# Prologue reordered, scratch stores moved into the prologue and two periods, y stores on GpSimd's queue, in an eight-core encoder layer

## The chip, the cores and the metric

One Trainium2 chip, all 8 of its cores. Every core runs the same program on two prompt streams (2 x 4096 rows) and two sample streams (32 rows in all), without exchange between cores. The metric is the device time of one execution, that of the slowest core, in microseconds (us).

## The reference, cut to what matters

```python
def trunk_layer(x, ..., cache_k, cache_v):            # D_MODEL 1024, one layer
    h = rms_norm(x, n_pre_mix)
    z = h @ w_in                                      # 1024 -> 5632: q | k | v | u,v of gMLP | gate_a | gate_b
    q, k, v, zg, ga, gb = split(z)
    a = sink_attention(q, k, v)                       # 64-row chunks see 2 previous chunks and their own, 16 heads, 4 KV heads
    u, gv = split(gelu(zg), 2)
    gv = layer_norm(gv, ln_g, ln_b)
    bm = u * (tril(w_s) @ gv + b_s)                   # over chunks of 128 rows, 4 channel groups
    merged = sigmoid(ga) * (a @ w_attn_proj) + sigmoid(gb) * (bm @ w_gmlp_proj)
    x = x + rms_norm(merged @ w_out, n_post_mix)
    h2 = rms_norm(x, n_pre_ffn)
    g, up = split(h2 @ w_ffn_in, 2)                   # D_FF 2816
    x = x + rms_norm((silu(g) * up) @ w_ffn_out, n_post_ffn)
    return x, new_k, new_v, gv
```

All inputs and outputs are float32. The kernel multiplies in bfloat16 with float32 accumulation.

## The kernel before, in words

**Work.** A core's prompt rows are 16 tiles of 512 rows (4 blocks `b` of 128); the 32 sample rows are a seventeenth small tile, `smp`. `big` holds a tile's activations transposed, in 48 chunks of 128 features x 512 rows: C_H (normed input, 0), C_U (8), C_Q (16), gates C_GA and C_GB (24, 32), C_MG (40); the FFN activations take over 24 and up.

**Stages.** The loop over tiles (lines 1074 to 1183) is skewed: iteration i does, for tile i, the merge (16 units of 8 matmuls: attention projection with `s_wap`, gMLP projection with `s_wgp`), `s_wout`, the post-mix norm, FFN in and FFN out, and for tile i+1 the input norm, q/k/v, attention (spread between FFN units), u, gv, layer norm, the spatial gate, and the two gates. What tile 0 needs of these (and `smp`) is done ahead of the loop, in the prologue (lines 1029 to 1072): norm, q/k/v units, then gate units with attention spread over a planned span of 46 us, then gv of blocks 0 and 1, the u units, gv of blocks 2 and 3 and of `smp`, layer norm and spatial gate. A unit is 8 matmuls of 128x512 into one PSUM bank (UNIT = 1.71).

**Order.** Every piece of work is an event with a planned time: `dense` for matmul units, `ev` for the rest, both in `plan`. The list is sorted by that time and then emitted; it fixes the order of the instructions on every engine and in every queue, since each runs its own in order. Times are never waited for; waits come from the dependencies that `MK` tracks (lines 48 to 132).

**Weights.** 34 blocks of 128x8x512 (keys `s_win` 0 to 10, `s_wfi` 0 to 10, two each of `s_wap`, `s_wgp`, `s_wout`, and six `s_wfo`) pass through a ring of 6 slots. `wload` (367 to 388): use number n of a key loads the float32 input from GpSimd's queue with a cast to bfloat16 while n <= `store_use[key]`; at n == `store_use[key]` SyncE's queue also stores the slot to a bfloat16 scratch in HBM, a DMA that waits for the load's landing; later uses load the scratch from SyncE's queue. A next load is emitted when a block's last use frees its slot (lines 1193 to 1197). Lines 350 to 365 set `store_use` by position in the order of use, cyclically from (0, 2, 1, 3, 1, 2), plus 1 for `s_win`, whose first use is the prologue; LAST_CAST is 3.

**Queues.** SyncE: scratch loads and stores, all loads of x, constants. GpSimd: cast loads, and DMAs of `YQ`. `YQ` (421) is the queue that stores y and small outputs: ACT until the end of iteration LAST_CAST, then GpSimd (line 1180). From there on `TQ` is true too: `norm_T` (469) transposes the normed rows by a DMA from ACT's queue, in place of 8 PE transposes into bank 0 and a copy by ACT. x of tile i+2 is loaded 18 planned us after `fo_fin` of the block (line 1149) into the slot of `xt` from which y was stored, so its DMA waits for that store.

**Attention.** `plan_attn` (651) makes for each pair (block, half of the heads) events for scores and exp (`attn_S`: ACT reads banks 1 and 2 into `PT`), `attn_PV` (590: matmuls into BO and BD, DVE adds the sinks into `dent`), two reciprocals of 128x256 on DVE (626), and `attn_fin` (631), a DVE multiply that reads BO and so frees it for the next pair.

**Result.** `fo_fin` (904) adds the normed FFN output into `xt` in place (POOL for the first half, DVE for the second) and stores y from there.

**Start.** Line 970: ACT scales `gS[:, 0, :]`, after its load. Lines 972 to 974: GpSimd's queue loads the K/V cache, ahead of the first ring loads. `consts_a` (980) loads constants, among them the sinks, `w_s`, `bsB` and `b16`; `consts_use` (993) makes `bs16` from `b16` and `es2` on DVE, planned three units before the end of q/k/v.

## Time and profile before

| what | us |
|---|---|
| device time, median of 3 runs | 4430.7 (4227.88 to 4873.92) |
| the profiled execution: device time | 4223.91 |
| its span on the slowest core (core 7) | 4222.4 |
| spans of the 8 cores | 4210.5 to 4222.4 |
| busy on core 7: PE, DVE, ACT, POOL | 4081.1, 2029.5, 1720.8, 1273.3 |

The span is from the first to the last instruction of one core. PE is TensorE's matmul, PEld its weight load, DVE VectorE, ACT ScalarE, POOL GpSimd, SP SyncE; SPq is SP's queue. PEclk is TensorE's granted clock, 1.00 being the higher of its levels (2.4 GHz), 0.5 the lower (1.2 GHz); a mean lies between. q0 is the queue of GpSimd's DMAs, q1 that of SyncE's, q10 that of ACT's. A DMA's bytes are those it writes, so a cast load of a 2 MB float32 block counts 1 MB.

### The profile page before, as it was taken

How to read it: one execution, taken by the hardware profiler on the slowest of the kernel's cores; microseconds unless marked ns; L12 is line 12 of the kernel's file. 1: busy time of each engine (PE TensorE's matmuls, PEld its weight loads, DVE VectorE, ACT ScalarE, POOL GpSimd, SP SyncE). 2: the span in 40 equal slices, each digit the busy share in tenths (PEclk: the TensorE clock that was granted, in tenths of full speed). 3: DMA queues.
4: the chain of work that ended last, by engine and by line, in shares of the span. 5: the costliest groups of instructions: out<-in, count | busy, mean ns of one | idle time of the engine just before them, and what ended most of it. 6: DMA issues, size and time to landing. Idle time of an engine off the chain costs nothing.

```text
span 4222.4 us, 63031 instructions; the slowest of 8 cores (4210.5 to 4222.4 us)
## 1 busy us (share of the span) xinstructions
PE 4081.1 (97%) x20672; PEld 1836.0 (43%) x20672; DVE 2029.5 (48%) x2849; ACT 1720.8 (41%) x3385; POOL 1273.3 (30%) x1294
## 2 busy tenths in 40 slices
PE   6799899999999999999999999999999999999988
PEld 3344444444444444444444444444444444444444
DVE  3555353554545545454554545445454554545332
ACT  3453352543525344352433525344252534435232
POOL 0233332332223322322332233232322332232242
PEclk9899999999999999999999999999999999999999
DMA  9487978767465463645537364553635546364422
GB/s 167 102 162 144 215 176 189 207 169 222 148 211 156 152 193 117 217 142 185 160 132 217 123 205 147 180 169 133 211 129 189 158 151 193 118 217 143 166 91 96
DMA packets 197727, 696.94 MB, mean 165 GB/s; under 512 B 105121, under 2 KB 105698, under 8 KB 127778
## 3 DMA queue, kind: packets, MB, share of 16 engines
q1 hardware_dynamic: 80258, 535.68, 36.5%
q0 software_dynamic: 21744, 125.58, 15.7%
q10 hardware_dynamic: 95408, 31.67, 4.4%
q8 instruction: 174, 2.85, 0.3%
q14 instruction: 143, 1.17, 0.1%
HBM read 699.88 MB, written 69.99 MB: 182 GB/s over the span
## 4 chain that ended last, share of the span: by engine, by line
PE 82%; DVE 6%; DMA 4%; issue 3%; ACT 2%; POOL 2%; DVEq 0%; ACTq 0%; SPq 0%; POOLq 0%
PE ps L310 82%; DMA big<-hst 1%; POOL stt L327 1%; DVE tmpf L338 1%; ACT junk L317 1%; DVE stt L705 1%; DVE hst L338 1%; DMA tmpf<-b_s 1%; DMA xt<-xp 1%; DVE gvn L338 1%; DVE gvf L338 1%; DVE xt L327 1%; DMA ring<-s_wap 0%; DMA ring<-wgp 0%; PE ps L476 0%
## 5 line engine op out<-in xcount | busy, mean ns | idle before, releaser
L310 PE MATMUL ps<-big,ring 128*128 128x512 bf16 x12032 | 2682.0, 381 | 7.1 <-DMA ring<-s_wap 3.6
L310 PEld LDWEIGHTS ps<-big,ring 128*128 128x128 bf16 x12032 | 1151.3, 98 | 1441.2 <-issue 118.1
L310 PE MATMUL ps<-ring,big 128*128 128x512 bf16 (+1 forms) x5376 | 1143.0, 369 | 24.7 <-POOL big L327 11.5
L327 POOL TENSOR_TENSOR big<-tmpf 128x512 bf16<-128x512 f32 x480 | 621.8, 1295 | 1664.4 <-ACT tmpf L322 1069.4
L310 PEld LDWEIGHTS ps<-ring,big 128*128 128x128 bf16 x5376 | 518.4, 98 | 587.6 <-issue 44.4
L315 ACT ACTIVATE big<-ps 128x512 bf16<-128x512 f32 (+1 forms) x552 | 341.8, 627 | 621.6 <-PE ps L310 452.8
L338 DVE SCALAR_TENSOR_TENSOR tmpf<-tmpf,ps 128x512 f32<-128x512 f32 x352 | 241.9, 687 | 608.6 <-ACT tmpf L315 608.6
L315 ACT ACTIVATE y<-ps 64x256 bf16<-64x256 f32 (+3 forms) x1024 | 488.6, 478 | 56.6 <-PE ps L310 3.0
L629 DVE RECIPROCAL dent<-dent 128x256 f32<-128x256 f32 (+1 forms) x264 | 441.2, 1692 | 9.2 <-DVE dent L327 0.5
L338 DVE SCALAR_TENSOR_TENSOR tmpf<-big,ps 128x512 f32<-128x512 bf16 x256 | 175.4, 686 | 535.6 <-PE ps L310 533.9
L327 POOL TENSOR_TENSOR stt<-stt,negh 128x1 f32<-128x1 f32 x320 | 226.7, 710 | 605.0 <-DVE stt L331 443.1
L322 ACT ACTIVATE tmpf<-ps 128x512 f32<-128x512 f32 (+1 forms) x355 | 212.0, 597 | 321.9 <-PE ps L310 198.6
L315 ACT ACTIVATE tmpf<-ps 128x512 f32<-128x512 f32 x352 | 210.1, 597 | 286.4 <-PE ps L310 279.9
L317 ACT ACTIVATE junk<-ps 128x512 bf16<-128x512 f32 x260 | 155.2, 597 | 408.8 <-PE ps L310 341.2
L317 ACT ACTIVATE junk<-xt 128x1024 bf16<-128x1024 f32 (+1 forms) x130 | 137.1, 1054 | 351.0 <-DVE tmpf L338 247.4
L315 ACT ACTIVATE gvf<-ps 128x512 f32<-128x512 f32 (+1 forms) x130 | 77.5, 597 | 381.5 <-PE ps L310 380.0
L705 DVE BATCH_NORM_STATS2 stt<-gvf 128x6 f32<-128x512 f32 (+1 forms) x130 | 87.8, 687 | 261.9 <-ACT gvf L315 261.9
L327 POOL TENSOR_TENSOR big<-tmpf,big 128x512 bf16<-128x512 f32 x128 | 146.7, 1160 | 210.3 <-DVE tmpf L327 210.1
L338 DVE SCALAR_TENSOR_TENSOR hst<-xt,stt,gS 128x1024 bf16<-128x1024 f32 (+1 forms) x130 | 167.5, 1289 | 59.0 <-DMA big<-hst 37.0
L327 POOL TENSOR_TENSOR xt<-xt,tmpf 128x512 f32<-128x512 f32 (+1 forms) x130 | 165.4, 1272 | 97.5 <-DVE tmpf L338 97.4
L327 DVE TENSOR_TENSOR xt<-xt,tmpf 128x512 f32<-128x512 f32 (+1 forms) x130 | 160.8, 1237 | 14.6 <-DVE tmpf L338 1.6
L338 DVE SCALAR_TENSOR_TENSOR tmpf<-ps,stt,gS 128x512 f32<-128x512 f32 (+1 forms) x195 | 140.0, 745 | 21.5 <-POOL stt L327 21.2
(94 smaller groups left out, 1550.4 us busy)
## 6 DMA issues: line engine op xcount, KB each, us to landing
ring<-s_wfi SPq DMA_DIRECT2D x148, 1024.0 KB, 6.0
ring<-s_win SPq DMA_DIRECT2D x138, 1024.0 KB, 5.9
ring<-s_wfo SPq DMA_DIRECT2D x54, 1024.0 KB, 4.9
ring<-w_in POOLq DMA_DIRECT2D x38, 1024.0 KB, 13.7
xt<-xp SPq DMA_DIRECT2D x64, 512.0 KB, 12.1
ring<-s_wap SPq DMA_DIRECT2D x29, 1024.0 KB, 10.7
ring<-wfi POOLq DMA_DIRECT2D x28, 1024.0 KB, 10.0
ring<-s_wout SPq DMA_DIRECT2D x27, 1024.0 KB, 6.4
```

The costliest lines, as they stand in the source:

```text
L310: m.op(PE, lambda e: e.matmul(out, lhsT=lhsT, rhs=rhs, start=start, stop=stop), reads=reads, writes=[("ps", b)])
L315: m.op(ACT, lambda e: e.activation(out=out, in_=in_, func=func, scale=scale), reads=reads, writes=writes)
L317: m.op(ACT, lambda e: e.activation(out=out, in_=in_, func=func, scale=scale, accum_out=accum_out), reads=reads, writes=writes)
L322: m.op(eng, lambda e: e.activation(out=out, in_=in_, func=AF.Copy), reads=reads, writes=writes)
L327: m.op(eng, lambda e: e.tensor_tensor(out=out, in0=in0, in1=in1, op=op), reads=reads, writes=writes)
L338: m.op(eng, lambda e: e.scalar_tensor_tensor(out=out, in0=in0, scalar=scalar, in1=in1, op0=op0, op1=op1), reads=reads, writes=writes)
L629: m.op(DVE, lambda e: e.reciprocal(out=dv, in_=dv), reads=[("dent", n % 2, h)], writes=[("dent", n % 2, h)])
L705: m.op(DVE, (lambda hh: lambda e: e.bn_stats(out=stt[0:P, c + 6 * hh:c + 6 * hh + 6], in_=gvf[0:P, g, hh * 512:(hh + 1) * 512]))(hh), read ...
```

## The change

- `store_use`: 8 keys (`s_win` 3 to 6, `s_wap`, `s_wgp`) are stored at their first use, 9 in iteration 0, the other 17 in iteration 1. LAST_CAST becomes 1; with it line 1180 sets `TQ` (DMA transposes) two iterations earlier.
- `YQ` is GpSimd's queue from the start.
- Prologue: attention is planned over the gate units' span alone; ACT copies BO to `tmpf` after PV, and POOL multiplies from there; gv of two blocks is followed by four u units, twice, with gv of `smp` before the last four; layer norm is placed after each gv block, the spatial gate after the u units that it multiplies. Normed gv of blocks 2 and 3 goes to `hst`, that of `smp` to `junk`. Copies after the transposes of blocks 1 and 3, and the gate multiplies of those blocks, go to DVE.
- `gS[:, 0, :]` is scaled on DVE, planned after the first two blocks' statistics. The cache loads are an event of the plan, and so stand behind the first six ring loads.

`fo_fin`, which adds in place, is not touched.

```diff
-        use_order = [(w, cb) for cb in range(2) for w in ("s_wap", "s_wgp")] + [("s_wout", 0), ("s_wout", 1)]
...
-        STORE_PERIOD = (0, 2, 1, 3, 1, 2)
-        LAST_CAST = max(STORE_PERIOD)
+        keys = [(w, cb) for w in ("s_wap", "s_wgp", "s_wout") for cb in range(2)]
+        keys += [(w, cb) for w in ("s_win", "s_wfi") for cb in range(11)]
+        keys += [("s_wfo", n, c) for n in range(2) for c in range(3)]
+        LAST_CAST = 1
+        in_prologue = {("s_win", cb) for cb in range(3, 7)} | {(w, cb) for w in ("s_wap", "s_wgp") for cb in range(2)}
+        in_first = {("s_wout", 1), ("s_win", 0), ("s_win", 2), ("s_wfi", 2), ("s_wfi", 5), ("s_wfi", 8),
+                    ("s_wfo", 0, 1), ("s_wfo", 1, 0), ("s_wfo", 1, 2)}
...
-            n = STORE_PERIOD[o % 6] + (1 if key[0] == "s_win" else 0)
+            n = 0 if key in in_prologue else (0 if key in in_first else LAST_CAST) + (1 if key[0] == "s_win" else 0)
...
-        YQ = [ACT]
+        YQ = [POOL]
         TQ = [False]
+        PRO = [True]
...
-            act(t["big"][:, c0:c0 + 8, b * P:(b + 1) * P], pTv[:, 0:8 * P].rearrange("p (k t) -> p k t", k=8), AF.Copy,
-                [("ps", pT_b)], BK(t, c0, c0 + 8, (b,)))
+            tcopy(DVE if PRO[0] and b % 2 else ACT, t["big"][:, c0:c0 + 8, b * P:(b + 1) * P],
+                  pTv[:, 0:8 * P].rearrange("p (k t) -> p k t", k=8), [("ps", pT_b)], BK(t, c0, c0 + 8, (b,)))
...
+            if PRO[0] and not sample:                      # end of attn_PV
+                ti = ntmp()
+                t["ao"][n] = ti
+                tcopy(ACT, tmpf[:, ti, :], banks[BO][:, :], [("ps", BO)], [("tmpf", ti)])
...
+            if n in t["ao"]:                               # attn_fin
+                ti = t["ao"][n]
+                tt(POOL, a_out, tmpf[:, ti, :].rearrange("p (g q) -> p g q", g=4),
+                   dv.rearrange("p (g q) -> p g q", g=4), ALU.mult,
+                   [("tmpf", ti), ("dent", n % 2, 0), ("dent", n % 2, 1)],
+                   BK(t, C_Q + 4 * tp, C_Q + 4 * tp + 4, (b,)))
+                return
...
+        def gn_of(t, b):                                   # where the normed gv of a block lies
+            g = b % 2
+            if t["sample"]:
+                return junk[:, :], ["junk", "junk"]
+            if t["own"] == 0 and b >= 2:
+                return hst[:, g, :], [("hst", g)] * 2
+            return gvn[:, g, :], [("gvn", g, 0), ("gvn", g, 1)]
...
-            tt(PX[0], uv, tmpf[:, ti, :].rearrange("p (j t) -> p j t", j=nj), uv, ALU.mult, [("tmpf", ti)] + uk, uk)
+            px = DVE if PRO[0] and b % 2 else PX[0]
+            tt(px, uv, tmpf[:, ti, :].rearrange("p (j t) -> p j t", j=nj), uv, ALU.mult, [("tmpf", ti)] + uk, uk)
...
-        act(gS[:, 0, :], gS[:, 0, :], AF.Copy, [("gS", 0)], [("gS", 0)], scale=32.0)
         m.fence([POOL], [k for b in range(4) for k in xk(b)])
-        for s_ in range(2):
...
+        def load_cache():
+            for s_ in range(2):
...
+        ev(0.0, load_cache)
+        ev(2.2, lambda: ts(DVE, gS[:, 0, :], gS[:, 0, :], 32.0, None, ALU.mult, None, [("gS", 0)], [("gS", 0)]))
...
-        e_at = plan_attn(t, s0 + 0.1, 46.0, smp)
-        u_end = now[0] + 12 * UNIT + 8 * SC
-        for b in range(2):
-            for hh in range(2):
-                dense(gv_unit(t, b, hh), UNIT)
-            plan_ln(t, b, now[0], u_end + 0.1 + 2.0 * b)
-        both(u_units(t), u_units(smp), 8)
-        for b in range(2, 4):
-            for hh in range(2):
-                dense(gv_unit(t, b, hh), UNIT)
-            plan_ln(t, b, now[0])
-        for hh in range(2):
-            dense(gv_unit(smp, 0, hh), UNIT)
-        e_sp = plan_ln(smp, 0, now[0] + 2.0)
+        e_at = plan_attn(t, s0 + 0.1, now[0] - s0, smp)
+        uu, us = u_units(t), u_units(smp)
+        for k in range(2):
+            for b in (2 * k, 2 * k + 1):
+                for hh in range(2):
+                    dense(gv_unit(t, b, hh), UNIT)
+                ev(now[0] + 0.1, (lambda b: lambda: ln_a(tiles[0], b))(b))
+                ev(now[0] + 2.1, (lambda b: lambda: ln_b_step(tiles[0], b))(b))
+            if k:
+                for hh in range(2):
+                    dense(gv_unit(smp, 0, hh), UNIT)
+                ev(now[0] + 0.1, lambda: ln_a(smp, 0))
+                ev(now[0] + 2.1, lambda: ln_b_step(smp, 0))
+            both(uu[4 * k:4 * k + 4], us[4 * k:4 * k + 4], 4)
+            for b in range(2 * k + 2):
+                if k == 0 or b >= 2:
+                    ev(now[0] + 0.1 + 0.2 * b, (lambda b: lambda: spatial(tiles[0], b, 0))(b))
+                if k == 1:
+                    ev(now[0] + 1.1 + 0.2 * b, (lambda b: lambda: spatial(tiles[0], b, 1))(b))
+        ev(now[0] + 2.0, lambda: spatial(smp, 0, 0))
+        e_sp = now[0] + 2.1
         ev(now[0], consts_b_use)
         not_before(max(e_at, e_sp) + 0.1)
+        ev(now[0], lambda: PRO.__setitem__(0, False))
```

## Rows read from the trace of the kernel before

**Rows 1.** The page, part 1: busy us (share of the span) xinstructions

```profile
PE 4081.1 (97%) x20672; PEld 1836.0 (43%) x20672; DVE 2029.5 (48%) x2849; ACT 1720.8 (41%) x3385; POOL 1273.3 (30%) x1294
```

**Rows 2.** Windows: start:end, length, busy of each engine (x), PEclk, DMA share, GB/s

```profile
21.50:68.20 46.70, 36.77 (x284) 20.04 (x284) 11.27 (x27) 18.18 (x40) 1.59 (x3) 1.00 1.02 168
68.20:152.00 83.80, 67.12 (x400) 28.29 (x401) 49.27 (x70) 48.71 (x108) 4.00 (x8) 0.85 0.66 142
152.00:191.50 39.50, 27.93 (x206) 13.90 (x203) 22.80 (x39) 11.81 (x24) 13.34 (x16) 0.85 0.53 90
191.50:264.00 72.50, 68.55 (x372) 33.41 (x370) 36.53 (x55) 26.05 (x48) 29.94 (x33) 0.97 0.75 134
...
378.00:648.70 270.70, 256.51 (x1283) 115.53 (x1282) 125.90 (x173) 111.39 (x210) 89.08 (x97) 0.98 0.86 183
648.70:912.95 264.25, 254.46 (x1280) 114.50 (x1278) 125.01 (x173) 111.04 (x210) 83.79 (x87) 0.99 0.79 195
912.95:1170.35 257.40, 253.10 (x1281) 114.25 (x1280) 124.71 (x173) 110.83 (x210) 77.68 (x76) 1.00 0.59 177
...
1672.07:3929.33 2257.26, 2240.99 (x10935) 998.57 (x10934) 1122.38 (x1550) 926.41 (x1812) 680.97 (x650) 1.00 0.51 166
```

**Rows 3.** Timeline of the prologue: start, length, instruction [idle before <-what ended it]

```profile
14.36 1.28 ACT L315 ACT_TABLE_LOAD   x1 [14.36 <-DMA gS<-g]
...
31.98 3.33 PE L310 MATMUL ps<-big,ring 128*128 128x512 bf16 x8
...
66.22 0.21 DVE L324 CAST bs<-tmpf 1x128 bf16<-1x128 f32 x1 [8.11 <-DMA tmpf<-b_s]
...
68.23 0.59 PE L310 MATMUL ps<-y,ones 128*64 128x512 bf16 x2 [3.83 <-DVE Vt L324]
...
190.87 0.18 PE L310 MATMUL ps<-WmT,gvn 32*128 32x32 bf16 x1 [6.45 <-DVE gvn L324]
```

**Rows 4.** Groups by form on ACT, 60 to 165 us: busy us, mean ns

```profile
L315 ACT ACTIVATE y<-ps 64x512 bf16<-64x512 f32 x28 | 16.5, 590 | 1.8 <-PE ps L310 0.3
...
L315 ACT ACTIVATE y<-ps 64x256 bf16<-64x256 f32 x28 | 10.6, 378 | 2.8 <-PE ps L310 1.2
L315 ACT ACT_TABLE_LOAD x8 | 10.3, 1283 | 6.4 <-PE ps L310 3.3 <-issue 3.0
```

**Rows 5.** Groups by form on DVE, 60 to 165 us

```profile
L629 DVE RECIPROCAL dent<-dent 128x256 f32<-128x256 f32 x16 | 27.4, 1732 | 1.1 <-DVE dent L327 0.5
```

**Rows 6.** The page, part 5: nearest rows to the moved multiply and copy

```profile
L322 ACT ACTIVATE tmpf<-ps 128x512 f32<-128x512 f32 (+1 forms) x355 | 212.0, 597 | 321.9 <-PE ps L310 198.6
...
L327 POOL TENSOR_TENSOR big<-tmpf,big 128x512 bf16<-128x512 f32 x128 | 146.7, 1160 | 210.3 <-DVE tmpf L327 210.1
```

**Rows 7.** Timeline of PE in iterations 0, 1 and 2

```profile
209.50 0.61 PE L476 MATMUL ps<-ident,hst 128*128 128x128 bf16 x8 [0.41 <-DVE hst L338]
...
482.77 1.01 PE L476 MATMUL ps<-ident,hst 128*128 128x128 bf16 x8 [8.06 <-DVE hst L338]
...
741.73 3.42 PE L310 MATMUL ps<-big,ring 128*128 128x512 bf16 x8 [3.56 <-DMA ring<-s_wap]
```

**Rows 8.** Timeline of SP's queue, around the starts of iterations 1 and 2

```profile
429.35 0.33 SPq L141 DMA_DIRECT2D xt<-xp  x1
456.25 0.32 SPq L141 DMA_DIRECT2D s_wap<-ring  x1
456.77 1.70 SPq L141 DMA_DIRECT2D xt<-xp  x3
...
719.49 0.32 SPq L141 DMA_DIRECT2D s_wgp<-ring  x1
```

**Rows 9.** The page, part 3: queue: packets, MB, share of 16 engines' span

```profile
q1 hardware_dynamic: 80258, 535.68, 36.5%
q0 software_dynamic: 21744, 125.58, 15.7%
```

**Rows 10.** DMA from 400 to 420 us: a queue, and issues with median us to landing

```profile
q0 software_dynamic: 410, 2.82, 92.9%
...
ring<-w_in POOLq DMA_DIRECT2D x1, 1024.0 KB, 24.6
...
yp<-xt ACTq DMA_DIRECT2D x2, 512.0 KB, 18.0
```

More of the change, by code:

```diff
@@ L348, in reg @@
             f32_of[key], b16_of[key], store_use[key] = f, b, n
-        use_order = [(w, cb) for cb in range(2) for w in ("s_wap", "s_wgp")] + [("s_wout", 0), ("s_wout", 1)]
-        use_order += [("s_win", cb) for cb in range(3)] + [("s_wfi", cb) for cb in range(11)]
-        use_order += [("s_win", cb) for cb in range(3, 7)] + [("s_wfo", n, c) for n in range(2) for c in range(3)]
-        use_order += [("s_win", cb) for cb in range(7, 11)]
-        STORE_PERIOD = (0, 2, 1, 3, 1, 2)
-        LAST_CAST = max(STORE_PERIOD)
+        keys = [(w, cb) for w in ("s_wap", "s_wgp", "s_wout") for cb in range(2)]
[5 more added lines that the diff above has]
+                    ("s_wfo", 0, 1), ("s_wfo", 1, 0), ("s_wfo", 1, 2)}
         src_of = {"s_win": (w_in, s_win), "s_wfi": (wfi, s_wfi), "s_wap": (wap, s_wap), "s_wgp": (wgp, s_wgp),
                   "s_wout": (wout, s_wout), "s_wfo": (wfo, s_wfo)}
-        for o, key in enumerate(use_order):
+        for key in keys:
             f, b = src_of[key[0]]
-            n = STORE_PERIOD[o % 6] + (1 if key[0] == "s_win" else 0)
+            n = 0 if key in in_prologue else (0 if key in in_first else LAST_CAST) + (1 if key[0] == "s_win" else 0)
             if key[0] == "s_wfo":
@@ L720, in ln_b_step @@
                        ALU.mult, gk + [("st", c + 12), "lng"], gk)
-                dst, dk = (gvf, gk) if t["sample"] else (gvn, [("gvn", g, hh)])
-                stt_op(DVE, dst[0:P, g, cs], gvf[0:P, g, cs], stt[0:P, c + 15:c + 16], lnb[0:P, cs], ALU.mult,
+                nv, nk = gn_of(t, b)
+                dst, dk = (gvf[0:P, g, cs], gk) if t["sample"] else (nv[0:P, cs], [nk[hh]])
+                stt_op(DVE, dst, gvf[0:P, g, cs], stt[0:P, c + 15:c + 16], lnb[0:P, cs], ALU.mult,
                        ALU.add, gk + [("st", c + 15), "lnb"], dk)
@@ L725, in ln_b_step @@
                 m.dma(YQ[0], "st_gs", gs[:, :], gvf[0:P, g, :], reads=[("gvf", g, 0), ("gvf", g, 1)])
-                for hh in range(2):
-                    cs = slice(hh * 512, (hh + 1) * 512)
-                    tcopy(DVE, gvn[0:P, g, cs], gvf[0:P, g, cs], [("gvf", g, hh)], [("gvn", g, hh)])
+                tcopy(DVE, nv[0:P, :], gvf[0:P, g, :], [("gvf", g, 0), ("gvf", g, 1)], [nk[0]])
         def spatial(t, b, half):
@@ L736, in spatial @@
                 o = banks[b_][:, jj * P:(jj + 1) * P]
-                lhs = gvn[0:P, g, j * 128:(j + 1) * 128]
-                rk = [("gvn", g, j // 4)]
+                nv, nk = gn_of(t, b)
+                lhs = nv[0:P, j * 128:(j + 1) * 128]
+                rk = [nk[j // 4]]
                 if sample:
@@ L943, in build_program @@
             t["own"] = i % NT
-            for k in ("r", "ln", "wb", "sq", "fb"):
+            for k in ("r", "ln", "wb", "sq", "fb", "ao"):
                 t[k] = {}
```

5 lines of the change are left out of this document (2 added, 3 removed).

## The prediction, made before the changed kernel was run

> **What bounds the kernel now.** I read the page's busy times first. PE is busy 4081 of 4222 us [rows 1]: at most 141 us can be won by filling PE's gaps, so the question is where these lie. The windows by stage answer that. Nine iterations in the middle take 2257.26 / 9 = 250.8 us each, with PE busy 99% and the DMA engines 51% [rows 2]: nothing is to be had there, and the change leaves them alone. Iterations 1, 2 and 3 (cut at the first layer norm of the next tile) take 270.7, 264.25 and 257.4, that is 19.9, 13.4 and 6.6 above it, with DMA shares of 0.86, 0.79 and 0.59. The prologue runs from 21.5 to 191.5; in its last 123.3 us PE is busy 67.12 + 27.93 = 95.05, and at a mean granted clock of 0.85, so some 30% of that time lies at the lower level [rows 2]. The excess is thus in two places: about 40 us in three iterations, and PE idle or slow in the prologue.
>
> **Iteration 3 (and 2): TQ two iterations earlier.** Before, these two transpose on PE: 8 groups of 8 at 0.61 us [rows 7] are 4.9 us, the rest of the 6.6 is waiting around them. The DMA transposes that replace them run in all nine middle iterations, which include their price. Iteration 3 also loses its last 6 cast loads. It becomes a middle iteration: -6.6 (6 to 7).
>
> **Iteration 2.** Its 13.4 are the same 6.6 and a stall at the merge. SP's queue waited until 719.49 to store `wgp`, a block cast-loaded then [rows 8]; a scratch load of `s_wap` stood behind it, PE waited 3.56 us for that and ran the next 8 matmuls in 3.42 us, twice a unit, at the lower level [rows 7]: 5.3 us in all. After, no cast load or store is left in iteration 2. What comes late in its place: the stores of `s_win` 7 to 10 now all fall at the end of iteration 1, ahead of the scratch loads for this merge in SP's queue. If they hold as `wgp` did, up to 5.3 stays; I keep 2. -11.4 (8 to 13.4).
>
> **Iteration 1.** PE idles 8.06 us for the second block's norm [rows 7]. The cause is in SP's queue: x of block 0 goes out at 429.35, then the store of `s_wap` waits for its cast load until 456.25, and x of blocks 1 to 3 only goes behind it at 456.77 [rows 8]. After, `wap` and `wgp` were stored in the prologue, so four plain loads stand there, and the first store of iteration 1 (`wout` 0) comes behind the planned x loads. The PE transposes stay (6.6 above a middle iteration), so the floor is 257.4. I keep 1 us for late x: -12.3 (6 to 13.3).
>
> **DMA supply.** Cast loads: 11 in the prologue and 34, 28, 17, 6 in iterations 0 to 3 before (96); 11 and 30, 17, 0, 0 after (58). Stores: 6, 11, 11, 6 before; 4 in the prologue, then 13 and 17 after; 34 in both. Over the span q0 takes 0.157 x 4222 / 125.58 = 5.3 us of the DMA engines per MB, q1 0.365 x 4222 / 535.68 = 2.9 [rows 9]; under load a cast block takes 0.929 x 20 / 2.82 = 6.6 [rows 10]. With 4 MB of x and y, iteration 0 needs 30 x 5.3 + 4 x 2.9 + 13 x 2.9 + 11.6 = 220 us instead of 209, iteration 1 17 x 5.3 + 17 x 2.9 + 17 x 2.9 + 11.6 = 200 instead of 209. Both fit in some 257, so the stores hide, and iteration 0 is put at no gain or loss (0 to 2: at 191.5 it starts with the clock low, 0.97 over 72.5 us [rows 2], and my prologue still ends with a short wait). At 6.6 a cast load, iteration 0 would need 259, just full: the low end.
>
> **Prologue: start.** ACT's table load and first square wait 14.36 us for `gS`, and the first matmul of a unit starts at 31.98 [rows 3]. With the scaling on DVE, ACT squares x as it lands; then only `gS` (14.4) and its scaling (below 1.3) stand before the first scaled block, which saves the table load, a scaling and a square on ACT, and the copies alternate between ACT and DVE. I take 5 us. The ring's loads start ahead of the cache loads, 2.3 us earlier, so the weights follow; the cache comes behind six blocks, still ahead of its use. But DVE then waits for `b16` until 66.22, and PE for `Vt` behind it until 68.23 [rows 3]. The constants are issued when the norms are done, so I move that by the same 5: first PV at 63.2. If the constants don't land earlier (DMA share 1.02 in this window [rows 2]), the 5 us are lost here.
>
> **Prologue: the rest.** Before, a pair's PV could start only after two reciprocals of 1.73 us [rows 5] and the multiply that frees BO, with exps sharing ACT with gelu: 8 table loads, 10.3 us [rows 4]. After, an ACT copy (0.6) frees BO, a POOL multiply (1.2 to 1.3) follows off the path [rows 6], and attention ends with the gates: two table loads, -7.7 us. The copies add 8 x 0.6 = 4.8 to ACT, which still has 16 evictions of `t` and of `smp` and 27.1 us of exps [rows 4]: about 47 us for a phase that PE needs some 50 for, so ACT is late next there. The multiplies stand in POOL's queue ahead of the ring loads; each holds them as long as DVE is late with a reciprocal, a few us, against a ring of six. PE's work from first PV to merge: 95.05 busy, of which up to 30% of 123.3 = 37 us at the lower level; at full clock 95.05 - 18.5 = 76.5 if PE was busy all through these, 95.05 if never; I take 86. Of the 123.3 - 86 = 37 us lost, what stays? The tail: PE idles 39.5 - 27.93 = 11.6 in the last window [rows 2], most of all for the layer norm of `smp` (6.45 [rows 3]); four u units with `smp`'s (7.7 us) now stand between, which leaves 4, and I add 2 for banks held by queued DVE adds. Exps, reciprocals and the clock: 8. So the merge starts at 63.2 + 86 + 14 = 163, not 191.5: -28.3. Bounds: no gain at the start and 25 still lost, 68.2 + 86 + 25 = 179 (-12); 4 lost, 153 (-38).
>
> **The y stores.** Before, the first four tiles' stores went from ACT; each now costs POOL one issue and a wait for DVE's add, as in the middle iterations. "In-place result" changes nothing: `fo_fin` added in place before. The trace shows what waits on these stores: x of the tile after next needs the slot. At 400 to 420 a y store on ACT's queue took 18.0 us to land while q0 filled 92.9% of the engines, and a cast load in q0 24.6 [rows 10]. The Trainium skill, "DMA: Bandwidth & Descriptors", section on queues, rings and completion order, says that an engine takes turns between queue rows but consumes one row in ring order. By that rule a store in q0 stands behind the cast loads instead of sharing with them, which speaks against this move; the 18.0 against 24.6 agrees with it, and no row shows a y store in q0 beside cast loads.
>
> **Sum.** 28.3 + 0 + 12.3 + 11.4 + 6.6 = 58.6. Span 4222.4 - 58.6 = 4163.8, device time (1.5 above the span) 4165. Bounds: gains 12 + 0 + 6 + 8 + 6 = 32 give 4192, 38 + 2 + 13.3 + 13.4 + 7 = 73.7 give 4150. This is set against the profiled execution's 4223.91, near the lowest of the three runs shown (4227.88); their median, 4430.7, is 207 above it and no base for these rows.
>
> **Rivals.**
> A, late x. A y store in q0 lands like a cast load, 6.6 us later, x goes out as much later, and the stalls of iterations 1 and 2 stay whole, with SP's loads behind the x loads. For it: the 24.6. Against it: x of blocks 1 to 3 was 27 us late before, far more than 6.6. Gains 28.3 + 6.6 + 6.6: 4182.
> B, the prologue hardly gains, because ACT takes DVE's place: -12 instead of -28.3, 4181.
> C, slower. Stores wait in SP's queue for cast loads, and scratch loads behind them reach PE late: the 5.3 us that the store of `wgp` cost, at each of the 17 stores of iteration 1, is 90: 4165 + 90 = 4255. It decides above 58.6 / 5.3 = 11 such stalls. Against it: of 34 such stores before, two held PE up visibly, and iteration 1 has less DMA work than before.
> D, prologue at PE's floor: 63.2 + 76.5 = 140 (-51.8), and every other term at its end (35.7): gain 87.5, 4136.
>
> **How the numbers follow.** Forecast 0.66, A 0.11, B 0.11, C 0.04, D 0.08. The time is the forecast's, 4165. Its own range, 4150 to 4192, takes in A and B; for 8 in 10, and with rows of single executions, I reach to 4140 and 4210. About 2% (84 us, 4139) is what a measurement of this kernel can tell from no change. Faster by more: D, 0.08, and 0.01 of the forecast's low end. Slower by more needs over 4308, twice C's price: 0.02. Within 2%: 0.89.
>
> **What would show it.** Right: first unit near 27, first PV near 63, merge of tile 0 near 163 and two or three table loads in the attention; iterations 1, 2 and 3 near 258, 253 and 251; DMA transposes from iteration 2; no PE wait of over 4 us for a ring slot or x. Wrong: PV still waiting for DVE's reciprocals; iteration 1 above 265 with x behind y stores; SP's queue waiting over 20 us for cast loads with PE idle after it; iteration 0 longer, at a DMA share near 1.

## The result, and the profile after

| what | before | after |
|---|---|---|
| lowest device time, us | 4223.85 | 4182.72 |
| ratio after / before, 95% interval | | 0.9896 [0.9874, 0.9919] |
| the profiled execution, device time | 4223.91 | 4182.72 |
| its spans, slowest core (lowest) | 4222.4 (4210.5) | 4181.2 (4162.3) |

Some executions of any of these kernels take up to about 5000 us, with the cores of a die at a lower granted clock; only the others are compared here and below. The gain is 41 us, within 2%; the forecast was 58.6 and 4165, and the compared executions of the changed kernel took 4182.7, 4184.95 and 4185.4.

The page of the changed kernel, first line and part 1, beside [rows 1]:

```profile
span 4181.2 us, 62902 instructions; the slowest of 8 cores (4162.3 to 4181.2 us)
PE 4074.0 (97%) x20544; PEld 1828.4 (44%) x20544; DVE 2029.2 (49%) x2847; ACT 1697.0 (41%) x3368; POOL 1269.2 (30%) x1281
```

PE lost 128 matmuls (two iterations' transposes), but its busy time only 7 us: the gain is idle time. The windows by stage, core 4, columns as in [rows 2]; the cuts are the first PV (PE's first matmul with the attention's exps), the merge of tile 0, and the first layer norm of each next tile:

```profile
62.20:177.90 115.70, 97.76 (x623) 43.01 (x623) 67.23 (x100) 56.65 (x135) 24.04 (x27) 0.86 0.91 196
177.90:358.20 180.30, 176.51 (x896) 78.31 (x894) 91.68 (x113) 89.91 (x167) 63.88 (x68) 0.99 0.79 171
358.20:615.30 257.10, 253.08 (x1282) 114.23 (x1280) 124.84 (x173) 110.86 (x210) 85.58 (x90) 1.00 0.84 210
615.30:873.40 258.10, 252.53 (x1218) 111.54 (x1216) 125.55 (x173) 103.24 (x202) 78.47 (x77) 0.99 0.64 187
873.40:1123.80 250.40, 248.82 (x1218) 110.93 (x1216) 124.77 (x173) 103.02 (x202) 75.12 (x72) 1.00 0.51 166
```

Iterations 1 and 3 are where the forecast put them (257.1 for 258.4, 250.4 for 250.8). Iteration 2 took 258.1, not 252.8, and the merge starts at 177.9, not 163. That is one core. On core 2 the same stretch, first PV to merge, is 9.5 us shorter, with less PE busy time and a higher clock:

```profile
57.40:163.60 106.20, 91.25 (x623) 41.72 (x622) 66.94 (x100) 57.49 (x138) 24.02 (x27) 0.94 0.95 212
```

So all eight cores have to be read. The same marks on each core of both profiled executions, their means and the extremes (us):

| mark | before, mean (range) | after, mean (range) | change of the mean |
|---|---|---|---|
| first PV | 66.5 (65.5 to 68.2) | 58.7 (57.2 to 62.2) | -7.8 |
| first PV to merge | 121.0 (119.4 to 123.3) | 109.1 (106.2 to 115.6) | -11.9 |
| PE busy in it | 92.4 (90.4 to 95.1) | 92.8 (90.1 to 97.8) | +0.3 |
| iteration 0 (merge to layer norm) | 180.0 | 179.9 | -0.1 |
| iteration 1 | 269.2 (267.6 to 270.9) | 257.2 (257.1 to 257.7) | -12.0 |
| iteration 2 | 261.9 (257.5 to 264.6) | 254.4 (252.0 to 258.1) | -7.5 |
| iteration 3 | 257.5 | 250.8 (250.4 to 252.5) | -6.8 |
| the rest | 3059.1 (3058.1 to 3061.0) | 3058.8 (3054.9 to 3068.7) | -0.3 |
| span | 4215.2 | 4168.9 | -46.3 |

The stretch from first PV to merge doesn't hold quite the same work: by PE's records the changed kernel has 240 of the units' 128x512 matmuls in it (core 4), the kernel before 232 (core 7), one unit more, 1.7 us at the higher clock. The first PV comes a unit earlier in PE's order, and part of its 7.8 us is that.

The mean core gained 46.3; two cores stand out late after the change, core 4 (4181.2) and core 7 (4178.7), while six lie between 4162.3 and 4167.6, within 4 us of the forecast span of 4163.8. The time is the latest core's.

PE's timeline on core 4 beside [rows 3]:

```profile
26.37 3.59 PE L310 MATMUL ps<-big,ring 128*128 128x512 bf16 x8
...
62.24 0.50 PE L310 MATMUL ps<-y,ones 128*64 128x512 bf16 x2 [4.13 <-DVE Vt L324]
64.68 0.37 PE L657 MATMUL ps<-ident,ckb 128*128 128x128 bf16 x2 [1.40 <-DMA ckb<-ck]
70.63 0.37 PE L657 MATMUL ps<-ident,ckb 128*128 128x128 bf16 x2 [2.17 <-DMA ckb<-ck]
...
697.37 3.15 PE L310 MATMUL ps<-big,ring 128*128 128x512 bf16 x8 [2.46 <-DMA ring<-s_wap]
...
730.87 1.67 PE L310 MATMUL ps<-ring,big 128*128 128x512 bf16 x6 [2.38 <-POOL big L327]
```

The first unit starts at 26.4 (31.98 before). The two waits for `ckb`, the cache, are new: the cache no longer is ahead of its use. Waits for it came on four of the eight cores (0.9 to 4.1 us). What the new order took away are PE's waits for DVE between first PV and merge, here on core 7 before:

```profile
PE ps L310 <- DVE big L327: 7.8, 3, 3.3
PE ps L310 <- DVE gvn L324: 6.4, 1, 6.4
PE ps L310 <- DVE gvn L338: 3.3, 1, 3.3
```

None of the three is left; smaller waits for DVE stand in their place (5.2 us in all on core 4, of the kinds of which core 7 had 1.4 before). PE's waits for ACT's exps stayed, 8.7 us on that core before, and on core 4 after:

```profile
PE ps L310 <- ACT y L315: 8.1, 11, 1.2
```

ACT's groups by form, 62 to 178 us, beside [rows 4, 6]:

```profile
L322 ACT ACTIVATE tmpf<-ps 128x512 f32<-128x512 f32 x8 | 4.8, 597 | 6.1 <-PE ps L310 6.1
...
L315 ACT ACT_TABLE_LOAD x1 | 1.3, 1283 | 2.0 <-PE ps L310 2.0
```

Eight copies for 4.8 us, as reckoned, and one table load where eight were. SP's queue at the start of iteration 1, beside [rows 8], and PE's first transposes there, beside [rows 7]:

```profile
355.52 35.46 SPq L141 DMA_DIRECT2D s_wfo<-ring  x3
...
414.72 0.34 SPq L141 DMA_DIRECT2D xt<-xp  x1
...
431.38 4.24 SPq L141 DMA_DIRECT2D xt<-xp  x2
446.41 0.33 SPq L141 DMA_DIRECT2D s_wout<-ring  x1
...
453.75 0.61 PE L478 MATMUL ps<-ident,hst 128*128 128x128 bf16 x8 [0.41 <-DVE hst L338]
```

x of all four blocks has gone out by 436, ahead of the store of `s_wout`, and PE's wait of 8.06 us is one of 0.41. SP's queue at the start of iteration 2:

```profile
655.31 32.51 SPq L141 DMA_DIRECT2D s_win<-ring  x4
687.98 0.32 SPq L141 DMA_DIRECT2D ring<-s_wap  x1
```

The gates' four stores (`s_win` 7 to 10) take SP 32.5 us, since each waits for its cast load, and the first scratch load of the merge goes out only then; PE waits for it at 697.37, and at 730.87 for a product of POOL. Only cores 1, 3, 4 and 7 waited for these scratch loads (1.1 to 4.2 us in all); core 0 has none of it and 4.3 us of waits for POOL and ACT, and how the stores reach those was not followed. The queues, beside [rows 9], and then the DMA issues of 655 to 675, beside [rows 10]:

```profile
q1 hardware_dynamic: 85730, 575.00, 39.7%
q0 software_dynamic: 18752, 94.84, 11.0%
```

```profile
yp<-xt POOLq DMA_DIRECT2D x4, 512.0 KB, 18.5
ring<-w_in POOLq DMA_DIRECT2D x1, 1024.0 KB, 22.6
```

A y store in q0 took 18.5 us to land beside cast loads, against 18.0 from ACT's queue, but q0 filled less of the engines here (71.2%, there 92.9%); the first experiment compares like with like.

### The profile page after: what moved, and what is told of

Same layout as the page of the kernel before. It is cut to its first block, busy times and chain, and to the rows that moved or that the text cites. A ratio compares the mean times of both kernels' runs of the same rounds, so it can differ in the third digit from the quotient of the medians.

```text
span 4181.2 us, 62902 instructions; the slowest of 8 cores (4162.3 to 4181.2 us)
## 1 busy us (share of the span) xinstructions
PE 4074.0 (97%) x20544; PEld 1828.4 (44%) x20544; DVE 2029.2 (49%) x2847; ACT 1697.0 (41%) x3368; POOL 1269.2 (30%) x1281
## 4 chain that ended last, share of the span: by engine, by line
PE 86%; DVE 4%; issue 3%; DMA 3%; POOL 2%; ACT 2%; ACTq 0%; DVEq 0%; another core or an unknown queue 0%; POOLq 0%; SPq 0%
PE ps L310 86%; DMA ckb<-ck 1%; POOL stt L327 1%; ACT junk L317 1%; DVE stt L726 1%; DVE tmpf L338 1%; DVE hst L338 1%; DVE gvn L338 1%; DVE gvf L338 1%; DMA ring<-w_in 1%; POOL big L327 0%; DMA big<-hst 0%; ACT y L322 0%; DVE tmpf L327 0%; DMA xt<-xp 0%
## 5 line engine op out<-in xcount | busy, mean ns | idle before, releaser
L315 ACT ACTIVATE big<-ps 128x512 bf16<-128x512 f32 x512 | 300.8, 596 | 507.6 <-PE ps L310 467.5
```

The costliest lines, as they stand in the source:

```text
L315: m.op(ACT, lambda e: e.activation(out=out, in_=in_, func=func, scale=scale), reads=reads, writes=writes)
```

## The experiments

What each kernel gave. Merge and iterations are ranges over the eight cores of its profiled execution, for "small cache first" over cores 0 to 3. Where no interval stands, there were too few times for one.

| kernel | times, us | ratio to before [95%] | merge of tile 0 | it. 1 | it. 2 |
|---|---|---|---|---|---|
| y on ACT | 4182.2, 4189.9 | 0.9885 [0.9813, 0.9957] | 168.5-178.7 | 257.1 | 252.4-263.4 |
| stores alone | 4204.5 to 4210.9 (4) | 0.9946 [0.9915, 0.9978] | 184.1-191.2 | 257.2-257.6 | 255.8-272.9 |
| prologue alone | 4205.6, 4208.4 | | 163.2-175.7 | 267.8-273.2 | 257.6-264.8 |
| cache first | 4184.5 to 4187.6 (4) | 0.9885 [0.9833, 0.9936] | 165.1-171.9 | 257.1 | 253.8-262.5 |
| cache late | 4192.4 to 4200.0 (3) | 0.9932 [0.9909, 0.9954] | 176.2-186.4 | 257.1-257.6 | 252.8-266.7 |
| small cache first | 4175.7, 4180.1, 4185.4 | 0.9871 [0.981, 0.9932] | 161.8-170.7 | 257.1 | 254.6-273.4 |
| stores at use | 4190.4 to 4199.6 (3) | 0.991 [0.9862, 0.9958] | 162.1-177.8 | 257.1 | 257.8-277.3 |
| transposes late | 4185.9 to 4203.2 (4) | 0.9913 [0.9873, 0.9952] | 163.3-182.6 | 257.1 | 257.4-266.1 |
| gates in iteration 0 | 4189.0, 4189.6 | 0.9892 [0.9806, 0.9978] | 163.1-174.8 | 266.6-271.8 | 250.4-252.4 |
| gates in prologue | 4200.1 to 4216.8 (4) | 0.9952 [0.9931, 0.9973] | 198.4-206.1 | 257.1 | 250.4-252.1 |
| both | 4195.1, 4203.6 | | 191.2-198.6 | 257.1 | 250.4-252.4 |
| both, transposes early | 4224.9 to 4243.7 (3) | 1.0026 [1.0004, 1.0049] | 190.0-195.6 | 274.1-308.1 | 250.4-251.8 |
| both, constants first | 4174.3 to 4185.6 (5) | 0.9888 [0.9871, 0.9905] | 168.8-177.8 | 257.1 | 250.4-252.2 |
| gates, constants first | 4174.7, 4176.8 | 0.9882 [0.9858, 0.9906] | 164.8-176.9 | 257.1 | 250.4-252.4 |
| the changed kernel again | 4184.6 | | 160.7-174.8 | 257.1-257.4 | 253.7-259.9 |
| both, constants first, ACT | 4172.8, 4177.9, 4179.7 | 0.9881 [0.9857, 0.9905] | 163.7-171.8 | 257.1 | 250.4-254.4 |

**The change in parts.** "y on ACT":

```diff
-        YQ = [POOL]
+        YQ = [ACT]
```

> The changed kernel with one word undone: the y stores of tiles 0 and 1 (and the small outputs until then) go from ACT's queue again. Theory (the 20 us between the forecast 4165 and the measured 4185 lie in the prologue of the slowest core, 177.9 against 163.6 to 169.3 on the other seven, and in a store wait at the start of iteration 2): the y queue hardly matters, 4180 to 4190, iteration 2 within 3 us of the changed kernel's 252 to 258 by core. Rival (y stores stand behind the cast loads in q0, so x and the loads behind x come late): iterations 1 and 2 fall to 257 and 251, and the time to 4172 to 4178. In iteration 1 I expect no difference by either, since it is at 257.1 already.

Iteration 1 stayed at 257.1 and the times are the changed kernel's: the queue of the y stores does not show in the iterations. Over all cores those of tiles 0 and 1 landed in a median of 14.0 and 16.6 us from ACT's queue, 15.8 and 16.1 from q0. In the prologue it does show: the mean merge is at 173.8, not 167.8. `YQ` also stores the sample's normed gv (`gs`), and on ACT's queue that store holds ACT until DVE has made it; PE then waits for ACT. Core 4:

```profile
159.62 0.32 ACTq L141 DMA_DIRECT2D gs<-gvf  x1
160.04 0.60 ACT L315 ACTIVATE big<-ps 128x512 bf16<-128x512 f32 x1 [6.78 <-DVE gvf L338]
160.78 0.38 PE L310 MATMUL ps<-bigs,ring 128*128 128x32 bf16 x8 [4.45 <-ACT bigs L315]
```

PE has this wait of 4.5 us on every core, and in the changed kernel one of 0.4. "Stores alone" is the kernel before with the new store schedule (and with it DMA transposes from iteration 2) and `YQ = [POOL]`:

```diff
+            n = 0 if key in in_prologue else (0 if key in in_first else LAST_CAST) + (1 if key[0] == "s_win" else 0)
...
+        YQ = [POOL]
```

> The kernel before with only the new store schedule (LAST_CAST 1, so DMA transposes from iteration 2) and y on GpSimd's queue; the old prologue stays. Theory: iterations 1, 2 and 3 as in the changed kernel, 257, 252 to 258 and 250.5, prologue about 185 to 192 as before; gain 13 + 8 + 7 = 28, time 4194 to 4202. The new stores in the prologue's queue hold nothing. Rival (the stores in the prologue load the DMA engines and cost the prologue time): merge of tile 0 starts at 195 or later, time above 4204.

"Prologue alone" is the reverse, the changed kernel with the old schedule:

```diff
-            n = 0 if key in in_prologue else (0 if key in in_first else LAST_CAST) + (1 if key[0] == "s_win" else 0)
+            n = STORE_PERIOD[o % 6] + (1 if key[0] == "s_win" else 0)
```

> The new prologue and the y stores on GpSimd's queue stay, but the scratch stores and the transposes go by the kernel before's schedule (four iterations). Theory (the parts add up): iterations 1, 2 and 3 fall back to 267-271, 258-265 and 257.4 us, the merge of tile 0 lies where the changed kernel has it (164-178 by core), time 4205-4212. Rival (the eight stores that the change puts into the prologue crowd its cache loads): the ckb waits of 1-4 us in front of the first pairs go, the latest core merges near 166, and the time is 4195-4203.

The parts separate by stage: the stores bring iterations 1 and 3 to the changed kernel's marks and leave the prologue as before, some 15 us, where 28 were expected, 8 of them in iteration 2; the prologue's order brings the merge forward and leaves the iterations, some 17. Iteration 2 alone does not follow: its mean is 261.9 with the stores alone and 262.4 with the prologue alone, but 254.4 with both, and most of the 9 us by which the parts fall short of 41 is this; why is open. The mean merge is 169.0 with one store in the prologue ("prologue alone") and 167.8 with eight, so these cost nothing, although they raise the DMA share there from 0.71-0.80 to 0.91-0.98.

**The prologue's waits.** "Cache first" puts the cache loads back ahead of the ring's, "cache late" behind the eighth (its edit is shown):

```diff
+                if sum(uses.values()) == 8:
+                    load_cache()
...
-        ev(0.0, load_cache)
```

> The changed kernel with the four cache loads ahead of the first six ring loads, as they were before. In the changed kernel PE waited for the cache on four of eight cores, 0.9 to 4.1 us, and ran slow after it. Theory: no wait for the cache on any core; the ring loads start 2.3 us later, which the first weights have in hand; the latest merge start falls from 177.9 to 172 or below, time 4172 to 4181. Rival (the slowest core's prologue is late for other reasons, the constants or the exps): the wait goes, but the latest merge start stays above 174 and the time within 4180 to 4188.

> The opposite of the cache mend: in the changed kernel the cache loads go behind the eighth ring load, which waits for a slot, instead of behind the sixth. Theory (a wait of PE for the cache also lowers the granted clock behind it, so it costs more than its own length): waits for ckb of 6-15 us on all cores, granted clock of PV to merge 0.80-0.88, PV to merge 118-128, time 4192-4205. Rival (a wait costs its own length and the clock goes its own way): granted clock as in the changed kernel, 0.90-0.94 on most cores, PV to merge 106-110 plus the wait.

With the cache first no core waited for `ckb`, first PV to merge took 106.0 to 109.2 on every core, and the latest merge fell from 177.9 to 171.9; but the mean merge rose from 167.8 to 169.4 (PE waits 1.7 to 6.3 us for `Vt` instead), and the time did not move. With the cache late, core 0's waits of PE and its windows:

```profile
PE ps L659 <- DMA ckb<-ck: 11.6, 1, 11.6
```

```profile
64.00:80.00 16.00, 4.38 (x21) 1.77 (x22) 2.64 (x3) 0.69 (x2) 0.00 (x0) 0.50 1.00 171
80.00:100.00 20.00, 17.34 (x121) 7.35 (x118) 11.24 (x15) 14.70 (x38) 4.33 (x4) 0.93 0.70 195
```

The clock stands at its lower level (0.50) in the stretch of the wait and is at 0.93 in the next. Over the cores the wait for `ckb` was 10.1 us on average, first PV to merge 118.9 against 107.6 with the cache first, PE's busy time 93.9 against 92.6. The mean clock of the whole stretch is 0.84 to 0.89 and the time lay in the theory's range, but the lower level stands in and around the wait itself. A wait cost its own length and about 1 us of slower matmuls, which is the rival's account. "Small cache first" moves the cache behind the third ring load and prepares on DVE only what the attention needs:

```diff
+                if sum(uses.values()) == 3:
+                    load_cache()
...
+        ev(s0 + 5.0, consts_use_late)
```

> The cache loads go behind the third ring load in GpSimd's queue instead of behind the sixth, and of the small constants only those that the attention needs are prepared on DVE ahead of it (the spatial ones 5 us after the attention's start). Theory (late cache and DVE's queue ahead of the first pairs keep the slowest core's merge late): no PE wait for ckb, first PV near 57-59 on all cores, PV to merge 106-109 on all cores, latest merge 166-168, time 4172-4180. Rival (PE's weights or the clock set the prologue's end): latest merge stays above 172 or only trades places between cores, time 4180-4187.

The waits for `ckb` and `Vt` were gone on every core, and first PV to merge took 106.0 to 109.1 on cores 0 to 3. Core 0's iteration 2 took 273.4; two of its DMA transposes there landed in 20.8 and 29.4 us.

**Iteration 2.** "Stores at use" issues a store only after the block's first unit, so that SP never waits for a cast load; "transposes late" leaves those of iterations 2 and 3 on PE (its edit is shown):

```diff
-            if i == LAST_CAST:
+            if i == 3:
```

> The changed kernel, with each scratch store put into SyncE's queue after the first unit that uses the block instead of right behind its load; what is stored, and in which iteration, stays. Theory: at the start of iteration 2 the scratch loads of s_wap and s_wgp no longer stand behind stores that wait for the landing of s_win 9 and 10, so iteration 2 falls from 252 to 258 (by core) to 250 to 252 and SyncE's waits for landings of cast loads from about 500 us to below 100; time 4176 to 4181. Rival (the loads are late because the DMA engines are full there, not because of the order in the queue): iteration 2 stays above 253 on most cores and the time within 4182 to 4188.

> Only the switch to DMA transposes is put off: they begin with iteration 3's tile as late as in the kernel before, everything else is as in the changed kernel. Theory (the stall of iteration 2 is made by the crowd of stores, cast loads and scratch loads at its start, and the transposes on PE cost 6.6 us an iteration): iteration 2 takes 258-264, iteration 3 257.4, time 4190-4198. Rival (DMA transposes in the crowded iteration 2 make its stall, since a transpose lands late there): iteration 2 is no longer than 258 on every core, only iteration 3 loses 7, time 4186-4190.

The first made it worse. SP's waits and PE's, core 1, 600 to 880 us:

```profile
SPq L166 <- DMA s_win<-ring: 42.3, 4, 15.5
```

```profile
PE ps L310 <- ACT big L315: 15.0, 2, 8.5
PE ps L310 <- DMA ring<-s_wout: 5.4, 1, 5.4
```

The slots now wait for their stores, and the scratch loads for the slots; that is the 5.4. The 15.0 for ACT go with late DMA transposes (one landed in 28.8 us, the longest of core 4's iteration 2 in the changed kernel in 10.9). So this run does not tell whether SP's order or the crowd of transfers makes the stall. With late transposes iteration 2 took 257.4 to 266.1, up to 9 above the 257.1 of iteration 1 with its PE transposes: the stall is not made by the DMA transposes. "Gates in iteration 0" moves the four stores one iteration up:

```diff
+        in_first = {("s_win", 7), ("s_win", 8), ("s_win", 9), ("s_win", 10), ("s_wout", 1), ("s_win", 0), ("s_win", 2),
...
```

> The stores of s_win 7 to 10 are put into iteration 0 instead of the end of iteration 1 (21 casts again in iteration 1 instead of 17 fall to 13, iteration 0 stores 17). Theory (these four stores, queued in SP ahead of the scratch loads of iteration 2's merge, make iteration 2's stall): iteration 2 takes 250-252.5 on all cores, iteration 1 257-260, time 4175-4182. Rival (DMA crowding merely moves): iteration 1 gains what iteration 2 loses, sum of iterations 1 and 2 stays at 509-515, time 4181-4187.

Iteration 2 went to its floor and iteration 1 rose by 10 to 15, to a sum of 519.8 on average, above the rival's too: the stall moved with the stores and grew. SP's queue on core 6, then PE's wait:

```profile
391.28 34.24 SPq L141 DMA_DIRECT2D s_win<-ring  x4
425.71 0.32 SPq L141 DMA_DIRECT2D ring<-s_wap  x1
```

```profile
PE ps L310 <- DMA ring<-s_wgp: 4.7, 1, 4.7
```

"Gates in prologue" exchanges them for `s_win` 3 to 6, and "both" adds "small cache first":

```diff
-        in_prologue = {("s_win", cb) for cb in range(3, 7)} | ...
+        in_prologue = {("s_win", cb) for cb in range(7, 11)} | ...
```

> The prologue stores s_win 7 to 10 (the gates) in place of s_win 3 to 6, which are then stored in the middle of iteration 1; each stage has as many stores as in the changed kernel (8, 13, 17). Theory (iteration 2 stalls because SP waits at the end of iteration 1 for the last cast loads, in front of the scratch loads and x of iteration 2): iteration 2 takes 250.4-252.5 on all cores, iteration 1 stays at 257.1, time 4172-4182 by what the slowest core's prologue is. Rival (the mere number of transfers of iteration 1 makes the stall): iteration 2 stays at 252-262 on most cores, time 4182-4188.

> The exchange of the gates' stores together with the cache loads behind the third ring load and the small constants split. Theory (both stalls go): first PV 56-62, PV to merge 104-109, latest merge 163-171, iterations 1 and 2 at 257.1 and 250.4-252.5, time 4163-4173. Rival (the prologue's clock stays low on some core whatever the loads do): latest merge 175-181, time 4175-4183.

Iteration 2 fell to 250.4-252.4 on every core with the same number of stores in each stage: it is the place of these four blocks, whose cast loads move with their stores, that makes the stall. But the merge came later, by 27 us on average in "both" (194.9 for 167.8) and by 34 in "gates in prologue" (202.3). SP's queue in the prologue of "both", core 7, and PE's wait:

```profile
47.06 17.10 SPq L141 DMA_DIRECT2D s_win<-ring  x3
64.25 0.69 SPq L141 DMA_DIRECT2D es<-sinks  x1
```

```profile
PE ps L310 <- DVE Vt L324: 28.4, 1, 28.4
```

The gates' blocks are among the ring's first fill, so their stores were issued ahead of the small constants, which then went out at 64.25 instead of 26. It is SP's order at a third place. "Both, transposes early":

```diff
-            if i == LAST_CAST:
+            if i == 0:
```

> As the kernel with both mends, and the DMA transposes begin one iteration earlier, in iteration 1. Theory (a transpose on PE costs what it costs in iterations 2 and 3, 6.6 us an iteration): iteration 1 takes 250.4-252.5, time 6-7 under the kernel with both mends, 4157-4167. Rival (transposes land late while 17 cast loads run in the same iteration): iteration 1 takes 255-265, time the same as that kernel's or above.

The rival held: iteration 1 took 274 to 308. PE's waits on core 2, 350 to 640 us, and the DMA transposes' landing there:

```profile
PE ps L310 <- DMA big<-hst: 18.2, 2, 14.5
PE ps L310 <- ACT big L315: 17.2, 2, 15.6
```

```profile
DMA to landing us min/median/max: 7.7/13.3/33.7
```

Beside 17 cast loads a transpose landed in a median of 13.3 us (5.9 in a middle iteration of the changed kernel). Transposes on PE cost 6.6 us an iteration and are the cheaper ones there.

**Both mended.** The stores of the first fill are held until the constants are issued, in "both" ("both, constants first") and in "gates in prologue" ("gates, constants first"); beside them the changed kernel ran again:

```diff
+                    if st_wait[0] is None:
+                        store()
+                    else:
+                        st_wait[0].append(store)
...
         ev(e_n, consts_a)
+        ev(e_n, release_stores)
```

> As the kernel with both mends, but the gates' stores that the first fill of the ring brings are held until the small constants have been issued on SP. Theory (gates' stores ahead of the constants made the 24-30 us wait for Vt, and the prologue and iteration 2 are otherwise mended): first PV 56-62, PV to merge 104-110, latest merge 164-172, iterations 1 and 2 at 257.1 and 250.4-252.5, time 4164-4174. Rival (four more stores during the first pairs or the granted clock hold the prologue back): PV to merge 112-120 on several cores, time 4175-4185.

> Only the exchange of the gates' stores with the constants first, the cache loads as in the changed kernel. Theory: iteration 2 at 250.4-252.5 on all cores, latest merge 168-180 as in the changed kernel with its ckb waits of 0-4 us, time 4168-4180, that is 5-8 under the changed kernel. Rival (iteration 2's stall does not count in the time, since the latest core makes it elsewhere): time as the changed kernel's within 3 us.

> The changed kernel itself, on the same chip as the two kernels above. Theory (the time is the latest of eight cores, and which core is late changes with its cache loads and iteration 2): ckb waits on some cores, latest merge 168-182, iteration 2 from 250 to 265, time 4180-4190. Rival (the late core 4 of the first profile was an accident): latest merge 169, iteration 2 at 252-255, time 4170-4176.

Iteration 2 was mended without the 27 to 34 us in the prologue (mean merges 172.2 and 170.8, the changed kernel again 168.4), and five of the seven executions of the two kernels took 4174.3 to 4176.8, some 8 below the changed kernel (two took 4185.6). The exchange of the stores alone gave as much as both mends, so this is iteration 2. But first PV to merge took 112.4 to 119.4 in "both, constants first", 115.4 on average, where "both" had 110.0. ACT's wait on core 1, and the landings of the DMAs into `vs`: the two stores that it waits for are the longest, 39.8 and 40.0, the others are loads of `cv` on SP:

```profile
ACT tmpf L322 <- DMA vs<-tmpf: 13.2, 1, 13.2
```

```profile
DMA to landing us min/median/max: 28.2/34.4/40.0
```

`YQ` issues more than y: the sample's new keys and values go out of `tmpf` through it, and ACT's copy of BO needs a `tmpf` slot. Over all cores such a store took 19.9 to 32.6 us to land in the changed kernel, 5.6 to 11.9 from ACT's queue ("y on ACT"), and 30.3 to 40.1 here, with the gates' stores beside it: late enough to be waited for, 4.3 to 13.2 us by core. The last run puts `YQ` back:

```diff
-        YQ = [POOL]
+        YQ = [ACT]
```

> As the kernel with both mends and the constants first, but what YQ issues in iterations 0 and 1 and in the prologue (y, and the sample's new keys and values out of tmpf) goes from ACT's queue again. Theory (in GpSimd's queue the new keys and values land behind cast loads, 28-40 us after issue with the gates' stores beside them, and hold the tmpf slot that ACT's copy of BO needs): no ACT wait for the store of vs over 2 us, PV to merge 104-110, latest merge 164-172, iterations 1 and 2 as before that at 257.1 and 250.4-252.5, time 4166-4174 unless a transpose lands late in a later iteration. Rival (the granted clock and the gates' stores themselves lengthen the prologue): PV to merge stays at 112-119, time 4174-4182.

No ACT wait for that store is left, and the latest merge fell from 177.8 to 171.8 (mean 168.6). First PV to merge is 107.0 to 116.0, 111.4 on average: the wait for `gs` on ACT's queue is back (4.5 us of PE on every core, as in "y on ACT"), and part of the rival stands. Its lowest time, 4172.8, is the lowest of all. Its interval overlaps the changed kernel's, so the step from 0.9896 to 0.9881 is not shown by ratios alone.

## Why the prediction was right or wrong

**Direction and class: right.** 41 us of 4224 is within 2%, and the time lay in the range. The gain was forecast 17 us too large.

**Iterations 1 and 3: right, and for the reason given.** x of iteration 1 no longer stands behind the store of `s_wap`; 257.1 is the floor of 257.4, without the microsecond kept for late x. "Stores alone" gave the same, so the prologue has no part in it. Iteration 3 became a middle iteration. Iteration 0 at no change: right (180.0 to 179.9). Of the 13 stores reckoned for it the four of `s_wap` and `s_wgp` went out ahead of the merge; 7 stand in the stretch measured (core 4).

**Iteration 2: place right, size off.** The text named the stores of `s_win` 7 to 10 ahead of the scratch loads and kept "2" of 5.3 us. On the mean core 254.4 - 250.4 = 4.0 stayed, on the latest 7.7. The price of one `wgp` store was no bound: these are four stores, each behind a cast load, and x and the scratch loads queue up behind all of them. The prediction's own sign of being wrong, SP waiting over 20 us with PE idle after it, came true here (32.5 us, then 2.46). Moving only these four blocks took the stall away (250.4 on most cores); that it goes by SP's order, and not by the crowd of cast loads that moved with them, is argued from the rows and not shown apart.

**Prologue: the step that failed is "I take 86".** That was PE's work from first PV to merge, chosen between 76.5 (full clock all through) and 95.05 (none gained). It measured 92.8 on the mean core, with one unit more in the stretch, where it was 92.4 before, and 97.8 on core 4: the reordering shortened PE's idle time, and hardly the part of its matmuls that run at the lower level. Nor was 76.5 a floor: the lowest of any core in all runs is 88.2 at a granted clock of 0.97 (the changed kernel again, core 5), so 86 asked for nearly the full clock all through.

```profile
57.80:160.70 102.90, 88.17 (x624) 40.95 (x624) 67.01 (x100) 57.49 (x138) 24.07 (x27) 0.97 0.96 214
```

The 18.5 behind 76.5 supposed PE busy through all of its lower-level time, but in part of that PE idles ("cache late": 0.50 over 16 us with 4.4 of them busy). Idle time fell from 28.5 to 16.3, near the 14 forecast. Against that the start was better than forecast, first PV 58.7 on average for 63.2, with a unit less ahead of it and the constants out on SP at 26.0 on core 4 ("both" shows that they set it: out at 64.25, PE waits 28.4 us for `Vt`). Of core 4's 14.7 us after the forecast merge (177.9 against 63.2 + 86 + 14 = 163.2), 11.8 are PE busy longer than 86 and 3.9 idle beyond the 14, less 1.0 for the earlier first PV.

**"The cache comes behind six blocks, still ahead of its use": wrong** on four of eight cores. Its price is a few us on the core that waits longest ("cache late": a wait costs its length), so it is the smaller part of core 4's delay. What lowers the clock on one core and not on the next stays open: in the last run cores 0 and 5 waited for neither the cache nor `Vt`, and PE's waits between first PV and merge are the same on both to 0.1 us in each group, and yet core 0 (first line) ran the stretch at 0.87 and core 5 at 0.97:

```profile
55.80:171.80 116.00, 98.18 (x622) 43.39 (x622) 67.69 (x103) 57.73 (x138) 23.47 (x26) 0.87 0.94 201
56.60:163.70 107.10, 89.31 (x624) 41.17 (x624) 67.69 (x103) 57.59 (x138) 23.53 (x26) 0.97 1.00 223
```

**The rows of one core for the latest of eight: the error that joins these.** The forecast took the gain on core 7, the latest before by some 4 us over the mean merge. The new prologue has a wider spread over the cores (merges 163.6 to 177.9, where they lay between 185.1 and 191.5), and an unlucky core sets the end. The account: the mean core gained 46.3 instead of 58.6 (prologue 8.7 short, iteration 2 3.9 short, the rest near nothing), and the latest core stands 12.3 above the mean where it stood 7.2 before.

**The rivals.** A (y stores in q0 make x late): fell with "y on ACT" and with iteration 1 at its floor. B (ACT takes DVE's place) gave nearly the measured time, 4181, but not by its mechanism: PE's waits for ACT's exps are single ones of at most 1.2 us on core 4, in all no more than before (8.1 and 8.7), and one table load is left. C (stores in SP's queue): the mechanism is real, and the experiments made it cost 10 to 15 us in iteration 1 and 27 to 34 in the prologue; in the change as made it costs 4 to 8 in one place, not 90, because what stands behind most stores has slack: SP's 35.5 us for three `s_wfo` stores at 355.52 cost iteration 1 nothing. (4308 is 1.6 times C's 90 above 4165, not twice.) D (PE's floor): no, 76.5 was none.

**The queue of the small stores.** For y the move into q0 shows no price (15.8 and 16.1 us to land against 14.0 and 16.6). For the small stores of new keys and values it shows one, 19.9 to 32.6 us against 5.6 to 11.9. The Trainium skill, "DMA: Bandwidth & Descriptors", section "Queues, rings and completion order", says of the queues of SP and ACT that on each engine descriptors are consumed in ring order. The small stores in q0 land as if that held for GpSimd's queue too; the y stores do not show it. The prediction weighed the queue for y alone and missed what else `YQ` issues: keys and values, for which nothing waited in the changed kernel, and `gs`, which on ACT's queue would have cost PE 4.5 us.

## What to carry to other kernels

Before a wait in an in-order queue is moved, list what stands behind it at the new place: four stores that wait for their loads cost 4 to 8 us ahead of iteration 2's scratch loads, 10 to 15 ahead of iteration 1's, 27 to 34 ahead of the prologue's constants, and nothing where the next entries have slack. The same holds for an engine that computes and issues DMAs: ACT stood 6.8 us behind a store that waited for DVE. Where the time is the latest of several cores, read the marks of all of them and forecast the spread as a term of its own. Removing idle time before a matmul is worth that idle time; count on PE's busy time to shrink as well only where a row shows it.

## What was not expected of the hardware

In several runs one DMA transpose of a middle iteration, with no cast load near, landed far later than the others and lengthened that iteration on one core. In "both, constants first" on core 6 it was 270.5 instead of 252.2 on core 0; the landings of its `hst` transposes:

```profile
DMA to landing us min/median/max: 2.7/6.3/26.3
```

In the changed kernel one on core 7 landed in 18.7 us and DVE waited 11.3 for it, and "the changed kernel again" and the last run each had one on their latest core, so it sets the time of some executions. The one profile of the kernel before shows none; whether the change has a part in it was not tried.
